# Expert outputs added to X's rows in DRAM by an indirect DMA, instead of stored, gathered and added by VectorE

## The chip, the cores and the metric

The kernel runs on one core of one Trainium2 chip. The metric is device microseconds of one execution, the median of three runs.

## The reference

A two-layer trunk over x (1024 tokens by 1024 features, float32). Each layer has a mixer and then a mixture of experts:

```python
x = x + g1[:, None, :] * y                        # y: the mixer's output
h = modulate(rms_norm(x, norm_ffn_g[l]), sh2, sc2)
x = x + g2[:, None, :] * grouped_moe(h, ...)
# grouped_moe: 16 experts, each token goes to 2 of them with gates summing to 1
a = silu(t @ w_gate[e]) * (t @ w_up[e])           # 1024 -> 256
y = sum over the token's 2 experts of gate * (a @ w_down[e])
```

Behind layer 0's experts stands layer 1's mixer: RMS norm of x, modulation, and a 1024 to 2048 projection `w1` with a gated activation, a width-31 convolution, and so on. Behind layer 1's experts stands the final RMS norm and the output.

## The kernel before

X stays in on-chip memory, 128 partitions by 8 blocks of 1024 features; block b holds tokens 128b to 128b+127. Engines are programmed one by one and wait on semaphores; there is no planner, so each engine's own order is the order of its work.

**The expert stage.** The router gives each token two slots. Slots are grouped by expert and padded to tiles of 128, so `nt` tiles are run a layer. `TOKI` holds for each tile and partition the token of that slot. Per tile:

- POOL gathers the tile's 128 normalised rows from `xn_scratch` in DRAM into `XG` with an indirect DMA (L581), for tile t+1 as soon as TensorE has transposed tile t (semaphore `xtr`); `XG` is a single buffer.
- TensorE's loop body for tile t is, in this order: gate and up of tile t (L1005, 16 records), transposes of tile t+1 (L996, waits for the gather), down of tile t-1 (L1020), transposes of tile t's hidden rows (L1012).
- ScalarE and VectorE evict the transposes, VectorE multiplies (L1161), and `tile_out` (L1419, L1421) scales the down result by the slot's gate and by g2 into the single buffer `YS`. It waits until the previous content of `YS` has left (`y_out`).
- ScalarE's queue stores `YS` to `y_scratch` at the tile's place (L691).
- SP's queue loads the weights of the expert three ahead, 3 MB, when the buffer's last `down` is done (L439 to L441).

**The combine.** When all tiles are stored, POOL issues 16 indirect gathers (L607), two for each block, and VectorE adds each to X (`combine`). ScalarE takes sums of squares block by block (`rms_sums`, L651), and after four blocks a root; VectorE normalises (`rms_apply`, L1227, L1231); TensorE transposes a half of 512 tokens (L869), ScalarE and VectorE evict (`evict_ht`). Only when both halves are there does TensorE start `w1`'s 16 groups (L886; group n takes `w1_group(n)`, whose first two need the first half only). In layer 1 two roots of four blocks each stand before the output.

SP loads the first two `w1` weight pieces when the last `down` of layer 0 is done, and two more when the last gather has landed.

Of the kernel before, what the change touches and what calls it, by code (L numbers as in the profile page):

```python
# [15 lines left out]
P = 128  # L16
# [108 lines left out]
def emptied(g):  # L125

    return CONSUMER[:g + 1].count(CONSUMER[g])


def trunk(nc, i, out):  # L130
    with ExitStack() as ctx:
# [35 lines left out]
        TCUR = sb("TCUR", [P, 1], U32)  # L167
        RT = sb("RT", [1, 5 * MAXT], I32)
# [73 lines left out]
        def hv(n):  # L242
            return HTR[:, n, :]

        Y1, Y2 = ([HTR[:, 3 * n + b, :] for b in range(3)] + [R[:, 3 - n, b * D:(b + 1) * D] for b in range(4)]
                  for n in range(2))
        NY0, NY = 3, 7

        def y_of(b):

            return b if b < NY else NY0
# [11 lines left out]
        xn_dram = nc.dram_tensor("xn_scratch", (T, D), F32, kind="Internal").ap()  # L263
        y_dram = nc.dram_tensor("y_scratch", (MOST * P, D), F32, kind="Internal").ap()
# [38 lines left out]
        xup = sem("x_updated")  # L303
# [40 lines left out]
        c_in = [[[sem(f"combine_in{l}_{b}_{s}") for s in range(2)] for b in range(NB)] for l in range(NL)]  # L344
# [66 lines left out]
        def _(sp):  # L411
# [54 lines left out]
            sp.wait_ge(zeroed, 16 * (NH + 1))  # L466
            nt = experts(0)
            sp.wait_ge(dn[0], nt)
# [23 lines left out]
            for n in range(2):  # L492
                weights1(n)
# [6 lines left out]
            sp.wait_ge(c_in[0][NB - 1][1], 16)  # L500
# [10 lines left out]
            experts(1)  # L511
# [7 lines left out]
        def _(pool):  # L519
# [35 lines left out]
            rest = y_dram[LEAST * P:MOST * P, :].rearrange("(t p) d -> p t d", p=P)  # L555
            zeros = ZERO.unsqueeze(1).broadcast_to([P, MOST - LEAST, HT])

            for q in range(16):
                if q == 4:
                    for h in range(NH):  # L560
                        pool.dma_start(rest[:, :, HT * h:HT * h + HT], zeros).then_inc(zeroed, 16)
                    pool.dma_start(glu_dram.rearrange("(c p) t -> p c t", p=P)[:, :, 0:PADC],
                                   ZERO[:, 0:KC * PADC].rearrange("p (c t) -> p c t", c=KC)).then_inc(zeroed, 16)
                l, s = q // 8, (2, 5)[q // 4 % 2]
                n = 24 * l + 4 * s + q % 4
                pool.wait_ge(ada_fin, n + 1)
                pool.dma_start(g_dram[q // 4:q // 4 + 1, q % 4 * QW:(q % 4 + 1) * QW], BROW[q % NBROW]
                               ).then_inc(brow_out[q % NBROW], 16)

            for l in range(NL):  # L570
# [13 lines left out]
                pool.tensor_tensor(PSCR[:, l:l + 1], PSCR[:, 2:3], PSCR[:, 2:3], ALU.add).then_inc(held[l], 1)  # L584
                pool.tensor_copy(TCUR[:], TOKI[:, 0:1]).then_inc(cur_ok[l], 1)
                pool.wait_ge(cur_ok[l], 1)
                gather()
                with pool.Fori(0, nt) as t:
# [4 lines left out]
                    pool.wait_ge(held[l], t + 1)  # L593

                    pool.tensor_tensor(PSCR[:, l:l + 1], PSCR[:, 2:3], PSCR[:, 2:3], ALU.add).then_inc(held[l], 1)
                    gather()

                pool.wait_ge(zeroed, 16 * (NH + 1))
                pool.wait_ge(y_out[l], nt * 16 + 16)
                pool.wait_ge(xg_in[l], nt * 16 + 16)  # L600
                pool.wait_ge(held[l], nt + 1)
                pool.tensor_tensor(PSCR[:, l:l + 1], PSCR[:, 2:3], PSCR[:, 2:3], ALU.add).then_inc(held[l], 1)
# [22 lines left out]
        def _(act):  # L625
# [18 lines left out]
            def rms_sums(r, h):  # L644

                if r == 0:
                    act.wait_ge(xl[h], 16)
                for b in range(4 * h, 4 * h + 4):
                    if r:
                        act.wait_ge(xup, 8 * (r // 2 - 1) + b + 1)  # L650
# [17 lines left out]
            def experts(l):  # L668
# [13 lines left out]
                act.sem_inc(y_out[l], 16)  # L682
# [6 lines left out]
                def store(t):  # L689
                    act.wait_ge(ys_d[l], t + 2)  # L690
                    act.dma_start(y_dram[bass.ds(t * P, P), :], YS).then_inc(y_out[l], 16)  # L691
                hidden(0)
                with act.Fori(1, nt) as t:
                    hidden(t)
                    store(t - 1)
                store(nt - 1)
# [59 lines left out]
            for h in range(NH):  # L756
                rms_sums(2, h)
            for h in range(NH):
                evict_ht(2, 1, 0, h)
            for n in range(16):  # L760
# [4 lines left out]
                act.activation(SIG[n % 2], take(g)[:], ACT.Sigmoid,  # L765
                               bias=PT[:, COL_B1 + KC + ct:COL_B1 + KC + ct + 1]).then_inc(free["A"], 1)
            act.wait_ge(conv_ok, KC)
# [24 lines left out]
            rms_sums(4, 0)  # L792
            rms_sums(4, 1)
# [3 lines left out]
        def _(pe):  # L797
# [294 lines left out]
            transposes(2, 1)  # L1092
# [31 lines left out]
            for n in range(16):  # L1124
                c, h = w1_group(n)
                ht_ready(2, h)
# [24 lines left out]
        def _(dve):  # L1151
# [68 lines left out]
            def rms_apply(r, h):  # L1220
# [4 lines left out]
                for b in range(4 * h, 4 * h + 4):  # L1225
                    if r < 4:
                        dve.tensor_scalar(XN[h][:, b % 4, :], X[:, b, :], RSTD[:, b:b + 1], None,  # L1227
                                          ALU.mult).then_inc(xn_ok, 1)
                        continue
                    dve.wait_ge(small_in, 48)  # L1230
                    dve.scalar_tensor_tensor(out=OUTS[b], in0=X[:, b, :], scalar=RSTD[:, b:b + 1],  # L1231
                                             in1=FGB, op0=ALU.mult, op1=ALU.mult).then_inc(out_ok, 1)
# [22 lines left out]
            def route(l):  # L1255
# [74 lines left out]
                for s, oh in ((0, OH1), (1, OH2)):  # L1330
# [12 lines left out]
                                              op0=ALU.mult, op1=ALU.add))  # L1343
                q3 = [P, 16, MAXT]
# [3 lines left out]
                for s in range(TOPK):  # L1348
# [4 lines left out]
                    tt(q4[:, s], q4[:, s], TOKF[:].unsqueeze(2).broadcast_to([P, NB, MAXT]), ALU.mult)  # L1353
# [33 lines left out]
                dve.tensor_copy(TOKI[:], X0[:, 0:MAXT]).then_inc(tab_ok, 1)  # L1387
# [192 lines left out]
            for b in range(NB):  # L1580
                if b == 5:
                    rms_apply(2, 0)
                combine(0, b)
            evict_ht(2, 1, 0, 0)
            rms_apply(2, 1)
            evict_ht(2, 1, 0, 1)
            for n in range(16):
                c, h = w1_group(n)
                g = GROUPS["w1"] + 2 * n + 1
                dve.wait_ge(free["A"], emptied(g - 1))  # L1590
# [38 lines left out]
            experts(1)  # L1629
            for b in range(NB):  # L1630
                if b == 5:
                    rms_apply(4, 0)
                combine(1, b)
            rms_apply(4, 1)
# [23 lines left out]
```

## Time and profile before

| | |
|---|---|
| median of 3 runs | 1817.98 us |
| lowest, highest | 1814.69, 1820.83 us |
| span of the profiled execution | 1812.5 us |
| TensorE busy | 1533.8 us, 85% |
| VectorE busy | 856.0 us, 47% |
| POOL busy | 150.2 us, 8% |

No time apart from the span is given for the profiled execution; the median of the runs is 5.5 us above that span. Times in the trace count from the span's start. PE is TensorE, DVE is VectorE, ACT is ScalarE, POOL is GpSimd; a q behind the name is that engine's queue of DMA issues. PEclk is the share of full clock granted to TensorE.

### The profile page before, as it was taken

Reading aid. Unit: us, or ns where it says so; the run is one execution under the profiler, and the core shown is the slowest. Engines: PE = TensorE matmul, PEld = TensorE weight load, DVE = VectorE, ACT = ScalarE, POOL = GpSimd, SP = SyncE. Lnnn points to the kernel's source line nnn. Section 1 sums busy time; section 2 is a strip of 40 time slices with the busy share of each in tenths; the row PEclk is TensorE's granted clock in tenths of the full one; section 3 lists DMA queues with packets and bytes.
Section 4 is the critical chain, followed back from the end, with each engine's and each line's share of the span. In section 5 each row is a group of like instructions: output and inputs, shape, how many; then the busy total and the mean of one; then the engine's idle time right before and its main releaser. Section 6 shows DMA issues by size and latency. Waiting matters only on the chain.

```text
span 1812.5 us, 17004 instructions
## 1 busy us (share of the span) xinstructions
PE 1533.8 (85%) x5355; PEld 850.0 (47%) x5356; DVE 856.0 (47%) x1548; ACT 258.0 (14%) x507; POOL 150.2 (8%) x267
## 2 busy tenths in 40 slices
PE   3799999989955999999359989987997489999980
PEld 2684544458843444444134334432886344444430
DVE  3554686644243332232353999966224422223326
ACT  2210000001121111111130000005112011111112
POOL 2000000000000111011310000000001011011104
PEclk9999999999986999999769989998999599999995
DMA  9574066560143666794532335442004567556727
GB/s 334 160 279 154 25 217 210 169 202 1 47 181 121 231 221 219 268 327 155 189 128 65 99 91 131 105 107 81 1 1 163 186 221 281 200 189 238 281 80 280
DMA packets 196430, 300.79 MB, mean 166 GB/s; under 512 B 12021, under 2 KB 153425, under 8 KB 196384
## 3 DMA queue, kind: packets, MB, share of 16 engines
q1 hardware_dynamic: 169952, 205.94, 36.1%
q0 software_dynamic: 17696, 62.24, 9.5%
q10 hardware_dynamic: 8736, 31.99, 4.5%
q8 instruction: 30, 0.49, 0.1%
q14 instruction: 16, 0.13, 0.0%
HBM read 248.51 MB, written 51.53 MB: 166 GB/s over the span
## 4 chain that ended last, share of the span: by engine, by line
PE 63%; DMA 16%; DVE 13%; issue 2%; ACT 2%; SPq 1%; POOL 1%; DVEq 0%; POOLq 0%; ACTq 0%
PE bank L886 19%; PE bank L964 15%; PE bank L1005 13%; DMA W<-in_moe_w_down 12%; PE bank L1020 6%; DVE W L1183 3%; DVE R L1604 3%; PE bank L996 2%; DVE R L1161 2%; PE bank L1109 1%; DMA W<-in_ada_w 1%; PE bank L869 1%; DVE X L1161 1%; PE bank L1142 1%; PE bank L903 1%
## 5 line engine op out<-in xcount | busy, mean ns | idle before, releaser
L886 PE MATMUL bank<-HTR,W 128*128 128x512 f32 x1024 | 451.4, 599 | 7.2 <-DVE R L1591 7.2
L1005 PE MATMUL bank<-W,R 128*128 (+1 forms) x816 | 369.5, 606 | 31.0 <-DMA W<-in_moe_w_down 14.2
L886 PEld LDWEIGHTS bank<-HTR,W 128*128 128x128 f32 x1024 | 193.9, 192 | 244.6 <-issue 244.0
L1161 DVE TENSOR_TENSOR R<-bank,R 128x256 f32<-128x256 f32 (+1 forms) x91 | 49.3, 542 | 540.6 <-ACT R L686 339.0
L1005 PEld LDWEIGHTS bank<-W,R 128*128 128x128 f32 x816 | 153.0, 192 | 217.8 <-issue 213.8
L964 PE MATMUL bank<-W,R 128*128 128x256 f32 x1024 | 231.1, 385 | 9.0 <-ACT R L786 7.8
L964 PEld LDWEIGHTS bank<-W,R 128*128 128x128 f32 x1024 | 194.6, 193 | 38.6 <-ACT R L786 8.7
L1604 DVE SCALAR_TENSOR_TENSOR R<-R,PT 128x998 f32<-128x998 f32 (+21 forms) x152 | 195.1, 1284 | 5.4
L1020 PE MATMUL bank<-W,R 128*128 x408 | 187.1, 602 | 3.8 <-DVE R L1412 3.8
L1183 DVE SCALAR_TENSOR_TENSOR W<-W,CAB 128x256 f32<-128x256 f32 x308 | 149.3, 485 | 11.0
L1020 PEld LDWEIGHTS bank<-W,R 128*128 128x128 f32 x408 | 74.7, 193 | 79.7 <-issue 79.7
L1419 DVE SCALAR_TENSOR_TENSOR R<-bank,GSLOT,HTR 128x512 f32<-128x512 f32 x51 | 38.3, 750 | 123.4 <-PE bank L1020 123.4
L678 ACT ACTIVATE R<-bank,MC 128x128 f32<-128x128 f32 x212 | 79.9, 457 | 95.4 <-PE bank L996 95.4
L686 ACT ACTIVATE R<-bank 128x256 f32<-128x256 f32 x51 | 19.6, 385 | 494.0 <-PE bank L1005 494.0
L869 PE MATMUL bank<-IDENT,R 128*128 128x128 f32 x128 | 27.4, 378 | 63.6 <-DVE R L1227 45.7
L1395 DVE TENSOR_SCALAR R<-bank,MC 128x128 f32<-128x128 f32 x212 | 72.4, 403 | 18.2 <-PE bank L996 18.2
L1161 DVE TENSOR_TENSOR R<-R 128x512 f32<-128x512 f32 (+8 forms) x146 | 64.5, 462 | 24.6 <-ACT R L751 21.3
L996 PEld LDWEIGHTS bank<-IDENT,R 128*128 128x128 f32 x424 | 50.9, 144 | 42.5 <-issue 26.9
L996 PE MATMUL bank<-IDENT,R 128*128 128x128 f32 x424 | 56.8, 278 | 15.2 <-DMA R<-xn_scratch,TCUR 15.2
L964 PE MATMUL bank<-W,HTR 128*128 128x256 f32 x256 | 58.7, 388 | 2.4 <-ACT HTR L660 1.4
L869 PEld LDWEIGHTS bank<-IDENT,R 128*128 128x128 f32 x128 | 20.6, 193 | 72.4 <-issue 35.0
L581 POOL DMA_INDIRECT R<-xn_scratch,TCUR x53 | 52.1, 983 | 25.1 <-issue 24.2
(191 smaller groups left out, 945.6 us busy)
## 6 DMA issues: line engine op xcount, KB each, us to landing
W<-in_ada_w SPq DMA_DIRECT2D x48, 1024.0 KB, 11.6
W<-in_moe_w_gate SPq DMA_DIRECT2D x32, 1024.0 KB, 7.4
W<-in_moe_w_up SPq DMA_DIRECT2D x32, 1024.0 KB, 11.0
W<-in_moe_w_down SPq DMA_DIRECT2D x32, 1024.0 KB, 12.9
y_scratch<-R ACTq DMA_DIRECT2D x51, 512.0 KB, 7.5
W<-glu_scratch SPq DMA_DIRECT2D x48, 258.0 KB, 4.6
W<-in_conf_w SPq DMA_DIRECT2D x12, 1024.0 KB, 8.8
W<-in_hyb_w_in SPq DMA_DIRECT2D x10, 1024.0 KB, 12.9
```

What stands on the lines that cost most here:

```text
L581: return pool.indirect_dma_start(out=XG, out_offset=None, in_=xn_dram, in_offset=bass.IndirectOffsetOnAxis(ap=TCUR[:, 0:1], axis=0)).then_ ...
L678: ins = act.activation(XT[:, k, :], TB_[0][:, k * P:(k + 1) * P], ACT.Identity, bias=MC[:, l, 3, k:k + 1], scale=MC[:, l, 2, k:k + 1])
L869: ins = pe.transpose(TB_[q % 2][:, P * b:P * b + P], XN[h][:, b, P * k:P * k + P], IDENT[:])
L886: ins = pe.matmul(dst[:], lhs(k), rhs(k), start=(k == 0), stop=(k == kc - 1))
L964: ins = pe.matmul(dst[:, QW * b:QW * b + QW], src[:, k, t0:t0 + P], w[:, k, :], start=(k == 0), stop=(k == KC - 1))
L996: ins = pe.transpose(TB_[k // 4][:, P * (k % 4):P * (k % 4) + P], XG[:, P * k:P * k + P], IDENT[:])
L1005: ins = pe.matmul(M[0][:], XT[:, k, :], W[:, bass.ds(at + k * 2 * FE, 2 * FE)], start=(k == 0), stop=(k == KC - 1))
L1020: ins = pe.matmul(M[1 + h][:], AT[:, k, :], W[:, bass.ds(at + 2 * KC * FE + k * D + h * HT, HT)], start=(k == 0), stop=(k == 1))
L1161: return dve.tensor_tensor(o, a, b, op)
L1183: ins = dve.scalar_tensor_tensor(out=acc, in0=w[:, k, :], scalar=CAB[:, k, 0:1], in1=acc, op0=ALU.mult, op1=ALU.add)
L1395: ins = dve.tensor_scalar(XT[:, k, :], TB_[1][:, (k - 4) * P:(k - 3) * P], MC[:, l, 2, k:k + 1], MC[:, l, 3, k:k + 1], ALU.mult, ALU.add)
L1604: link(dve.scalar_tensor_tensor(out=o[:, d:T], in0=p[:, 0:T - d], scalar=tap(CTAPS - 1 - d), in1=o[:, d:T], op0=ALU.mult, op1=ALU.add))
```

## The change

`y_scratch` and its zero fill go. In their place `xsum_scratch` (`xs_dram`) holds a copy of X's rows: ScalarE stores four pieces of 1 MB while the mixer's output projection finishes. For each tile POOL issues an indirect DMA that adds `YS` onto the 128 rows of `xs_dram` that the tile's tokens name. This `add_rows(t - 1)` stands in POOL's loop behind `next_tile(t)`, which issues the gather of tile t+1. It waits for the previous add to have landed and for `tile_out`. Padding slots name a spare block of rows.

When the last add has landed, SP reloads X in eight blocks of 512 KB. The combine, its gathers and the `xup` semaphore are gone. Behind layer 0, SP loads the first two `w1` pieces after four of the eight reloads, and the transposes and evictions of the second half stand behind `w1`'s first two groups. Behind layer 1, root, scaling and output go block by block.

```diff
 # POOL, setup: the zero fill of y_scratch goes, a spare block of rows stays
-            rest = y_dram[LEAST * P:MOST * P, :].rearrange("(t p) d -> p t d", p=P)
-            zeros = ZERO.unsqueeze(1).broadcast_to([P, MOST - LEAST, HT])
...
+                        pool.dma_start(xn_dram[T:T + P, s], ZERO).then_inc(zeroed, 16)
+                        pool.dma_start(xs_dram[T:T + P, s], ZERO).then_inc(y_out[h], 16)
 # POOL, the expert stage
+                def next_tile(t):
                     pool.wait_ge(xg_in[l], t * 16 + 16)
                     pool.tensor_copy(TCUR[:], TOKI[:, bass.ds(t + 1, 1)]).then_inc(cur_ok[l], 1)
                     pool.wait_ge(cur_ok[l], t + 2)
                     pool.wait_ge(xtr[l], t + 1)
+                    met()
                     gather()
+                def add_rows(t):
+                    pool.wait_ge(y_out[l], t * 16 + 16)
+                    pool.tensor_copy(TSUM[:], TOKI[:, bass.ds(t, 1)]).then_inc(sum_cur[l], 1)
+                    pool.wait_ge(sum_cur[l], t + 1)
+                    pool.wait_ge(ys_d[l], t + 2)
+                    met()
+                    pool.indirect_dma_start(
+                        out=xs_dram, out_offset=bass.IndirectOffsetOnAxis(ap=TSUM[:, 0:1], axis=0),
+                        in_=YS, in_offset=None, compute_op=ALU.add).then_inc(y_out[l], 16)
...
+                next_tile(0)
+                pool.wait_ge(x_out[l], 16 * 4)
+                with pool.Fori(1, nt) as t:
+                    next_tile(t)
+                    add_rows(t - 1)
+                add_rows(nt - 1)
-                for b in range(NB):
-                    if b == NY:
-                        pool.wait_ge(xup, 8 * l + NY0 + 1)
-                    for s, dst in ((0, Y1), (1, Y2)):
-                        pool.indirect_dma_start(
-                            out=dst[y_of(b)], out_offset=None, in_=y_dram,
-                            in_offset=bass.IndirectOffsetOnAxis(ap=SLOTU[:, s, b:b + 1], axis=0)
-                        ).then_inc(c_in[l][b][s], 16)
 # ACT
-                def store(t):
-                    act.wait_ge(ys_d[l], t + 2)
-                    act.dma_start(y_dram[bass.ds(t * P, P), :], YS).then_inc(y_out[l], 16)
 # ACT, x_pieces: four stores a layer of X's rows, 1 MB each
+                    act.dma_start(xs_dram[2 * P * p:2 * P * (p + 1), :].rearrange("(b q) d -> q b d", q=P),
+                                  X[:, 2 * p:2 * p + 2, :]).then_inc(x_out[l], 16)
 # SP
+            def reload(l, nt, b):
+                if b == 0:
+                    sp.wait_ge(y_out[l], nt * 16 + 16)
+                sp.dma_start(X[:, b, :], xs_dram[P * b:P * b + P, :]).then_inc(x_back[b], 16)
-            sp.wait_ge(dn[0], nt)
...
-            for n in range(2):
-                weights1(n)
+            for b in range(NB):
+                reload(0, nt, b)
+                if b == 3:
+                    for n in range(2):
+                        weights1(n)
...
-            sp.wait_ge(c_in[0][NB - 1][1], 16)
...
-            experts(1)
+            nt = experts(1)
+            for b in range(NB):
+                reload(1, nt, b)
 # PE, ACT and DVE: the second half's transposes move behind the first two groups of w1
             transposes(2, 0)
-            transposes(2, 1)
             for n in range(16):
                 c, h = w1_group(n)
+                if n == 2:
+                    transposes(2, 1)
 # DVE, route: padding slots name rows T + p of the spare block, each its own
+                tokr = SM[:, 0:16].rearrange("p (s b) -> p s b", s=TOPK)
+                link(dve.tensor_scalar(SPARE[:], TOKF[:, 0:1], float(T), None, ALU.add))
+                for s in range(TOPK):
+                    dve.scalar_tensor_tensor(out=tokr[:, s, :], in0=TOKF[:], scalar=-float(T),
+                                             in1=rf.rearrange("p (s b) -> p s b", s=TOPK)[:, s, :],
+                                             op0=ALU.add, op1=ALU.subtract).then_inc(dch, 1)
...
-                dve.tensor_copy(TOKI[:], X0[:, 0:MAXT]).then_inc(tab_ok, 1)
+                dve.tensor_scalar(TOKI[:], X0[:, 0:MAXT], SPARE[:], None, ALU.add).then_inc(tab_ok, 1)
 # DVE, behind the experts
-            def combine(l, b):
-                for s, y in ((0, Y1), (1, Y2)):
-                    dve.wait_ge(c_in[l][b][s], 16)
-                    ins = tt(X[:, b, :], X[:, b, :], y[y_of(b)], ALU.add)
-                    if s == 0:
-                        link(ins)
-                ins.then_inc(xup, 1)
+            def last_norm(b):
+                dve.wait_ge(fin_sd, b + 1)
+                link(dve.reciprocal(RSTD[:, b:b + 1], SD[:, b:b + 1]))
+                dve.scalar_tensor_tensor(out=OUTS[b], in0=X[:, b, :], scalar=RSTD[:, b:b + 1],
+                                         in1=FGB, op0=ALU.mult, op1=ALU.mult).then_inc(out_ok, 1)
```

## Rows read from the trace of the kernel before

**Rows 1.** The page: the span, and TensorE's line of busy times.

```profile
span 1812.5 us, 17004 instructions
PE 1533.8 (85%) x5355; PEld 850.0 (47%) x5356; DVE 856.0 (47%) x1548; ACT 258.0 (14%) x507; POOL 150.2 (8%) x267
```

**Rows 2.** Busy time by stretch: 12 us of layer 0's expert stage.

```profile
core 0: us, PE busy (x) PEld busy (x) DVE busy (x) ACT busy (x) POOL busy (x), PEclk, DMA share, GB/s
648.00:660.00 12.00, 11.69 (x36) 5.62 (x35) 3.49 (x8) 1.89 (x5) 1.35 (x3) 1.00 1.00 349
```

**Rows 3.** Timeline, one tile: start us, us, engine, line, operation, count, [idle before].

```profile
649.64 1.04 PE L996 MATMUL bank<-IDENT,R 128*128 128x128 f32 x8
...
650.51 3.60 PE L1020 MATMUL bank<-W,R 128*128 x8
...
650.81 0.18 POOL L595 TENSOR_TENSOR PSCR<-PSCR 1x1 f32<-1x1 f32 x1 [6.72 <-PE bank L996]
651.46 0.98 POOL L581 DMA_INDIRECT R<-xn_scratch,TCUR  x1 [0.46 <-issue]
...
654.36 0.75 DVE L1419 SCALAR_TENSOR_TENSOR R<-bank,GSLOT,HTR 128x512 f32<-128x512 f32 x1 [2.28 <-PE bank L1020]
...
655.03 0.74 DVE L1421 SCALAR_TENSOR_TENSOR R<-bank,GSLOT,HTR 128x512 f32<-128x512 f32 x1
...
655.95 0.34 ACTq L691 DMA_DIRECT2D y_scratch<-R  x1
656.91 0.18 POOL L590 COPY TCUR<-TOKI 128x1 uint32 x1 [4.47 <-DMA R<-xn_scratch,TCUR]
661.61 0.60 PE L996 MATMUL bank<-IDENT,R 128*128 128x128 f32 x4
```

**Rows 4.** DMA issues: count, KB, median us to landing; then the landings of L581.

```profile
y_scratch<-R ACTq DMA_DIRECT2D x51, 512.0 KB, 7.5
...
R<-xn_scratch,TCUR POOLq DMA_INDIRECT x53, 4.5
...
DMA to landing us min/median/max: 4.0/4.5/7.6
```

**Rows 5.** The chain: gate-and-up of tile 1 and of the last tile, each layer.

```profile
582.81 7.13 PE bank L1005 x16
...
860.66 7.13 PE bank L1005 x16
...
1453.13 7.13 PE bank L1005 x16
...
1744.61 7.13 PE bank L1005 x16
```

**Rows 6.** Behind layer 0's experts: timeline, and last the chain.

```profile
880.54 0.74 DVE L1421 SCALAR_TENSOR_TENSOR R<-bank,GSLOT,HTR 128x512 f32<-128x512 f32 x1
...
907.50 1.06 ACT L651 ACTIVATE R<-X 128x1024 bf16<-128x1024 f32 x1 [2.64 <-DVE X L1161]
...
913.64 1.94 PE L869 MATMUL bank<-IDENT,R 128*128 128x128 f32 x8 [34.02 <-DVE R L1227]
...
933.55 6.62 PE L869 MATMUL bank<-IDENT,R 128*128 128x128 f32 x28 [3.77 <-DVE R L1227]
...
941.06 41.22 PE bank L886 x96
```

**Rows 7.** Behind layer 1's experts: timeline and chain.

```profile
1764.49 0.74 DVE L1421 SCALAR_TENSOR_TENSOR R<-bank,GSLOT,HTR 128x512 f32<-128x512 f32 x1
...
1765.41 2.67 DMA y_scratch<-R
```

**Rows 8.** Busy time by stretch, columns as in rows 2: two gaps of TensorE.

```profile
578.00:583.00 5.00, 1.57 (x12) 1.10 (x11) 2.05 (x6) 1.89 (x5) 1.16 (x2) 1.00 0.29 93
872.40:874.20 1.80, 0.00 (x0) 0.00 (x0) 1.69 (x3) 0.00 (x0) 0.00 (x0) 1.00 0.00 0
874.20:879.70 5.50, 5.39 (x8) 2.03 (x8) 0.00 (x0) 0.00 (x0) 0.00 (x0) 0.69 0.23 95
```

More of the change, by code:

```diff
@@ L167, in trunk @@
         TCUR = sb("TCUR", [P, 1], U32)
+        TSUM = sb("TSUM", [P, 1], U32)
+        SPARE = sb("SPARE", [P, 1])
         RT = sb("RT", [1, 5 * MAXT], I32)
@@ L243, in hv @@
             return HTR[:, n, :]
[L245 to L251, printed above, removed]
         GBF = hv(6)
@@ L260, in trunk @@
         X0, X1 = bank[6], bank[7]
-        xn_dram = nc.dram_tensor("xn_scratch", (T, D), F32, kind="Internal").ap()
-        y_dram = nc.dram_tensor("y_scratch", (MOST * P, D), F32, kind="Internal").ap()
+        xn_dram = nc.dram_tensor("xn_scratch", (T + P, D), F32, kind="Internal").ap()
+        xs_dram = nc.dram_tensor("xsum_scratch", (T + P, D), F32, kind="Internal").ap()
         g_dram = nc.dram_tensor("gate_scratch", (4, D), F32, kind="Internal").ap()
@@ L302, in trunk @@
         gb_in = [sem(f"gate_rows_in{n}") for n in range(4)]
-        xup = sem("x_updated")
         dch = sem("dve_step")
@@ L343, in trunk @@
         y_out = [sem(f"tile_stored{l}") for l in range(NL)]
-        c_in = [[[sem(f"combine_in{l}_{b}_{s}") for s in range(2)] for b in range(NB)] for l in range(NL)]
+        x_out = [sem(f"x_rows_stored{l}") for l in range(NL)]
+        x_back = [sem(f"x_block_reloaded{b}") for b in range(NB)]
+        sum_cur = [sem(f"sum_tokens_copied{l}") for l in range(NL)]
+        fin_sd = sem("final_root_ready")
         out_ok = sem("output_block_ready")
@@ L466, in _ @@
             sp.wait_ge(zeroed, 16 * (NH + 1))
+            for l in range(NL):
+                sp.wait_ge(y_out[l], 16)
+            def reload(l, nt, b):
+                if b == 0:
+                    sp.wait_ge(y_out[l], nt * 16 + 16)
+                sp.dma_start(X[:, b, :], xs_dram[P * b:P * b + P, :]).then_inc(x_back[b], 16)
             nt = experts(0)
-            sp.wait_ge(dn[0], nt)
             def weights1(n):
@@ L560, in _ @@
                     for h in range(NH):
-                        pool.dma_start(rest[:, :, HT * h:HT * h + HT], zeros).then_inc(zeroed, 16)
+                        s = slice(HT * h, HT * h + HT)
+                        pool.dma_start(xn_dram[T:T + P, s], ZERO).then_inc(zeroed, 16)
+                        pool.dma_start(xs_dram[T:T + P, s], ZERO).then_inc(y_out[h], 16)
                     pool.dma_start(glu_dram.rearrange("(c p) t -> p c t", p=P)[:, :, 0:PADC],
@@ L583, in gather, with met @@
                         in_offset=bass.IndirectOffsetOnAxis(ap=TCUR[:, 0:1], axis=0)).then_inc(xg_in[l], 16)
[L584 to L588, printed above, removed]
+                def met():
+                    pool.tensor_tensor(PSCR[:, l:l + 1], PSCR[:, 2:3], PSCR[:, 2:3], ALU.add).then_inc(held[l], 1)
+                def next_tile(t):
                     pool.wait_ge(xg_in[l], t * 16 + 16)
@@ L592, in _ @@
                     pool.wait_ge(xtr[l], t + 1)
-                    pool.wait_ge(held[l], t + 1)
-                    pool.tensor_tensor(PSCR[:, l:l + 1], PSCR[:, 2:3], PSCR[:, 2:3], ALU.add).then_inc(held[l], 1)
+                    met()
                     gather()
-                pool.wait_ge(zeroed, 16 * (NH + 1))
-                pool.wait_ge(y_out[l], nt * 16 + 16)
-                pool.wait_ge(xg_in[l], nt * 16 + 16)
-                pool.wait_ge(held[l], nt + 1)
-                pool.tensor_tensor(PSCR[:, l:l + 1], PSCR[:, 2:3], PSCR[:, 2:3], ALU.add).then_inc(held[l], 1)
-                for b in range(NB):
-                    if b == NY:
-                        pool.wait_ge(xup, 8 * l + NY0 + 1)
-                    for s, dst in ((0, Y1), (1, Y2)):
-                        pool.indirect_dma_start(
-                            out=dst[y_of(b)], out_offset=None, in_=y_dram,
-                            in_offset=bass.IndirectOffsetOnAxis(ap=SLOTU[:, s, b:b + 1], axis=0)
-                        ).then_inc(c_in[l][b][s], 16)
+                def add_rows(t):
[7 more added lines that the diff above has]
+                        in_=YS, in_offset=None, compute_op=ALU.add).then_inc(y_out[l], 16)
+                met()
+                pool.tensor_copy(TCUR[:], TOKI[:, 0:1]).then_inc(cur_ok[l], 1)
+                pool.wait_ge(cur_ok[l], 1)
+                gather()
+                next_tile(0)
[4 more added lines that the diff above has]
+                add_rows(nt - 1)
+                pool.wait_ge(xg_in[l], nt * 16 + 16)
                 if l == 0:
@@ L649, in rms_sums @@
                     if r:
-                        act.wait_ge(xup, 8 * (r // 2 - 1) + b + 1)
+                        act.wait_ge(x_back[b], 16 * (r // 2))
                     link(act.activation(JUNK, X[:, b, :], ACT.Square, accum_out=SS[:, b:b + 1]))
@@ L681, in experts @@
                 evict_tile(1)
-                act.sem_inc(y_out[l], 16)
                 def hidden(t):
@@ L694, in experts @@
                     hidden(t)
-                    store(t - 1)
-                store(nt - 1)
             def x_pieces(l, g0):
@@ L754, in _, with gate1 @@
             experts(0)
[L756 to L760, printed above, removed]
+            def gate1(n):
                 g = GROUPS["w1"] + 2 * n
@@ L766, in _ @@
                                bias=PT[:, COL_B1 + KC + ct:COL_B1 + KC + ct + 1]).then_inc(free["A"], 1)
+            rms_sums(2, 0)
+            evict_ht(2, 1, 0, 0)
+            rms_sums(2, 1)
+            for n in range(16):
+                if n == 2:
+                    evict_ht(2, 1, 0, 1)
+                gate1(n)
             act.wait_ge(conv_ok, KC)
@@ L791, in _ @@
             experts(1)
-            rms_sums(4, 0)
-            rms_sums(4, 1)
+            for b in range(NB):
+                act.wait_ge(x_back[b], 32)
+                link(act.activation(JUNK, X[:, b, :], ACT.Square, accum_out=SS[:, b:b + 1]))
+                act.activation(SD[:, b:b + 1], SS[:, b:b + 1], ACT.Sqrt, bias=EPSC[:],
+                               scale=1.0 / D).then_inc(fin_sd, 1)
         @block.tensor
@@ L1125, in _ @@
                 c, h = w1_group(n)
+                if n == 2:
+                    transposes(2, 1)
                 ht_ready(2, h)
@@ L1225, in rms_apply @@
                 for b in range(4 * h, 4 * h + 4):
[L1226 to L1232, printed above, removed]
+                    dve.tensor_scalar(XN[h][:, b % 4, :], X[:, b, :], RSTD[:, b:b + 1], None,
+                                      ALU.mult).then_inc(xn_ok, 1)
             def evict_ht(r, l, ffn, h, ks=range(1, KC, 2)):
@@ L1343, in route @@
                                               op0=ALU.mult, op1=ALU.add))
+                tokr = SM[:, 0:16].rearrange("p (s b) -> p s b", s=TOPK)
[4 more added lines that the diff above has]
+                                             op0=ALU.add, op1=ALU.subtract).then_inc(dch, 1)
+                    steps[0] += 1
                 q3 = [P, 16, MAXT]
@@ L1352, in route @@
                     dve.wait_ge(dch, steps[0])
-                    tt(q4[:, s], q4[:, s], TOKF[:].unsqueeze(2).broadcast_to([P, NB, MAXT]), ALU.mult)
+                    tt(q4[:, s], q4[:, s], tokr[:, s, :].unsqueeze(2).broadcast_to([P, NB, MAXT]), ALU.mult)
                 tt(RO, IOTA[:].unsqueeze(1).broadcast_to([P, 16, P]),
@@ L1578, in _ @@
             experts(0)
[L1580 to L1583, printed above, removed]
+            rms_apply(2, 0)
             evict_ht(2, 1, 0, 0)
             rms_apply(2, 1)
-            evict_ht(2, 1, 0, 1)
             for n in range(16):
@@ L1589, in _ @@
                 g = GROUPS["w1"] + 2 * n + 1
+                if n == 2:
+                    evict_ht(2, 1, 0, 1)
                 dve.wait_ge(free["A"], emptied(g - 1))
@@ L1629, in _ @@
             experts(1)
+            dve.wait_ge(small_in, 48)
             for b in range(NB):
[L1631 to L1634, printed above, removed]
+                last_norm(b)
 INPUTS = ["x", "c", "ada_w", "ada_b", "norm_mix_g", "norm_ffn_g", "hyb_w_in", "sgu_ln_g", "sgu_ln_b",
```

## The prediction

> **What bounds the kernel now.** I read the page first: TensorE is busy for 1533.8 of 1812.5 us [rows 1]. Then I took busy time by stretch. In the expert stage TensorE is all but full: 11.69 us of 12 at full clock, while POOL has 1.35 us of work [rows 2]. So the stage is bound by TensorE's own order of work, and anything that makes it wait once a tile costs once a tile.
>
> The timeline of one tile shows the slack that the change spends. TensorE transposes a tile at 649.64. POOL sees it at 650.81 and issues the next gather at 651.46, before the down of the tile is done. It has landed when POOL goes on at 656.91, and TensorE comes back for it at 661.61 [rows 3]: 4.7 us of slack. The store of `YS` is issued at 655.95 and lands in 7.5 us [rows 4], 663.4. VectorE wants the buffer again one period after 654.36, at about 666.3, which leaves 2.9 us.
>
> The period comes from the chain: 582.81 to 860.66 in 23 steps, and 1453.13 to 1744.61 in 24 [rows 5], together 569.3 us in 47 steps, 12.1 us each. The store's count is 51 [rows 4], so the layers have 25 and 26 tiles.
>
> Behind each expert stage the kernel is bound by a string of dependent work: 881.3 (end of the last `tile_out`) to 941.06 (first `w1` matmul) is 59.8 us in layer 0 [rows 6], and 1765.2 to the span's end at 1812.5 is 47.3 us in layer 1 [rows 1, 7]. This is what the change shortens.
>
> **What the change saves, layer 0.** The last `tile_out` still ends at 881.3. POOL then needs a wake-up, `met` and a pause: 0.13 + 0.18 + 0.47 = 0.78 us, as between the end of the transposes and the gather [rows 3]. The add is issued at 882.1. No accumulating DMA is in the trace. Below, the nearest row is the plain store of the same bytes with the queues empty, 2.67 us [rows 7]; above, the gather's longest landing, 7.6 [rows 4]. I take 5.0, near an indirect transfer's usual 4.5: landed at 887.1. The reloads follow. I take 2.7 us to the first landing (the same store) and then 1.5 us a block, since 0.524 MB at the 349 GB/s that the queues reach [rows 2] is 1.5. Block 3 is in at 887.1 + 2.7 + 4.5 = 894.3. From the start of that block's sum of squares to the first transpose takes 913.64 - 907.50 = 6.1 us [rows 6]: 900.4. A half of transposes with its evictions takes 941.06 - 933.55 = 7.5: 907.9. By then two pieces of `w1` (2 MB more, 6 us) are in as well, at about 900.3. Two groups of `w1` are two thirds of 41.22 us, 27.5 [rows 6]: 935.4. Now the second half's transposes, 7.5, and the third group, 13.7: 956.6. Before, the third group ended at 941.06 + 41.22 = 982.3. VectorE's convolution work starts there, and that work sets the pace next, so this is the point to compare. Saved: 25.7 us; from 20 (add 7.6, reload paced at two thirds of the rate) to 28 (add 2.7).
>
> **Layer 1.** The add is issued at 1765.2 + 0.8 = 1766.0 and lands at 1771.0. Eight loads and eight output stores of 0.524 MB are 8.4 MB, 24 us at 349 GB/s. The last store's landing adds some 2: the end is at 1797, 15.5 us earlier, from 11 to 19. Sum of the savings: 41 us.
>
> **Small items.** The four 1 MB stores of X fall under the projection, where TensorE has work and the queues little; I price them at nothing, and 3 us a layer (1 MB at 349 GB/s) if the last one delayed the rows that the first gather reads. The three more VectorE steps in the router are on the path, small ones, for which POOL's smallest of 0.18 us [rows 3] is the nearest row: under 1 us a layer. The removed zero fill ran beside TensorE's first projections and frees nothing that anyone waits for. Together +1 us.
>
> **What it costs in the loop.** POOL's order is now gather(t+1), add(t-1), gather(t+2). Add(t-1) must wait for `tile_out(t-1)`, that is for down(t-1), which TensorE does *after* transposing t+1. So gather(t+2), so far issued right behind the transposes, is now held behind down, `tile_out` and the issue of the add. The loop that closes, counted from the start of the transposes:
> - to the start of `tile_out`: 654.36 - 649.64 = 4.72
> - `tile_out`: 655.03 + 0.74 - 654.36 = 1.41
> - POOL wake-up, `met`, pause: 0.78
> - issue of the add, as the gather's: 0.98 (bounds half and twice that; no row shows this form)
> - end of the loop, copy to `TCUR`, `met`, pause: estimated at 1.25, from two small operations of 0.18, 0.47 of pause, and some 0.4 between them and for the branch
> - sum to the gather's issue: 9.1 us [rows 3]
> - gather to landing: L
> - and TensorE starts the next transposes.
>
> The period is 9.1 + L, where it used to be 12.1. L was 4.0 to 7.6, median 4.5 [rows 4], when the gather started ahead of the weights. Now it starts in their midst and right behind the add of the same size on its own queue. The store that started at that moment took 7.5. I take 7.5 for the 26 tiles beside a weight load (16 experts a layer, three of them loaded ahead of the loop) and 5.1 for the other 21: mean 6.4. Bounds 4.0 and 12 (below, the slow add).
>
> TensorE then idles some 4 us a tile. After 1.8 us without work the clock was granted at 0.69 over the next 5.5 us, and the eight `down` records in it took 5.39 us [rows 8] in place of 3.60 [rows 3]. But in 578 to 583, with 1.57 of 5 us busy, it stayed at 1.00 [rows 8]. The transposes and `down` behind the gap are on the closed loop. I take half of 5.39 - 3.60 = 1.8: 0.9; bounds 0 and the rival below. The Trainium skill has a rule for this (*TensorE: Matmul & The Clock Gate*, section "HAM oscillation — how this bites in real kernels"): idle gaps once an iteration make the array start each one at the low clock. By it every tile would pay; the two gaps here agree once and once not.
>
> Period: 9.1 + 6.4 + 0.9 = 16.4, that is 4.3 more. Adds stand ahead of the gathers of tiles 3 to nt, nt - 2 periods a layer: 23 + 24 = 47. 47 x 4.3 = 202 us. The wait of `tile_out` for the previous add stays hidden: it has 16.4 - 2.2 = 14.2 us. The weights have more room than before.
>
> **Sum.** +202 - 41 + 1 = +162 us. From the profiled span, 1812.5 + 162 = 1974.5; with the 5.5 us by which the median lies above it, **1980 us**. The savings are worth 41 / 47 = 0.87 us a tile: the loop decides.
>
> **The rivals.**
> 1. *Only the order costs.* The add and the weights don't slow the gather, L = 4.5, and the clock holds. For it: landings keep near 4.5 beside weights in most tiles. Against: the store's 7.5 at just this moment. Period 13.6, +71 - 40 = +31: 1849 us.
> 2. *The clock falls every tile.* At the low level eight transposes take 1.94 us [rows 6] against 1.04 [rows 3], 0.9 more, and down 1.8 more: 2.7 in place of 0.9. Period 18.2, +287 - 40: 2065 us. This is the page's rule in the rows' numbers.
> 3. *The adding DMA itself is slow.* If it needs 12 us, 1.6 times the busy store's 7.5 [rows 4], and the gather lands 1.3 us behind it, the period is 6.9 + 12 + 1.3 + 0.9 = 21.1, +423, and each layer's savings shrink by 7: +397, 2215 us. For it: it must read its target and write it. The Trainium skill (*Collectives: The Full Stack*, "The bandwidth ceiling: the fold count and why AG ≠ RS ≠ AR") says that a reducing transfer runs at about half rate, since it reads two sources; by that alone the add's 1.5 us of transfer would be 3, an estimate, and no run here shows it.
> 4. *The other side: the gather stays hidden.* It needs 9.1 + L at 12.1 or less. If POOL came to the gather 1.1 us sooner than I counted and L were its shortest 4.0, nothing would stall, and the savings stand: 1818 - 41 = 1777 us. It decides for faster when the period stays below 12.1 + 0.87 = 13.0. Against: 9.1 is nearly all measured rows, and 4.0 is the minimum of 53 gathers that had nothing ahead of them.
>
> **How the numbers follow.** Forecast 0.44 (own range 1910 to 2045, L from 5 to 7.5 with its clock share); rival 1 0.16; rival 2 0.19; rival 3 0.16; rival 4 0.05. A change within 0.3%, some 5 us, is what a measurement of this kernel can't tell from none: it needs a period of 12.9 to 13.1, 0.02 of rival 4. Slower 0.95, same 0.02, faster 0.03. Range: from rival 1 with a little less L, 1845, to short of the slow add, 2165; outside lie rival 4 and most of rival 3.
>
> **What would show it.** Right: TensorE's idle time ahead of L996, released by the gather, 3 to 6 us a tile where it is now none; gates-and-ups some 16.4 us apart; the gather issued at about 9.1 us behind the transposes, right behind the add; PEclk below 1.00 in parts of the stage; 51 adds. Also the first `w1` matmul 26 us after the last `tile_out` and not 60, and some 32 us from the last `tile_out` to the end. Wrong: gates-and-ups still 12 us apart; or the wait found at `tile_out` for the add, not at the transposes; or an add whose issue takes many us on POOL.

## The result, and the profile after

The changed kernel takes 2107.18 us (median of 4 runs, 2104.51 to 2110.3) against 1819.4 for the kernel before (median of 4 here); the ratio is 1.159, interval 1.1568 to 1.1611. It is 288 us slower. I had said 162 us slower, 1980 us, range 1845 to 2165.

The page of the changed kernel, span and TensorE:

```profile
span 2108.5 us, 17096 instructions
PE 1611.2 (76%) x5355; PEld 890.8 (42%) x5356; DVE 819.4 (39%) x1528; ACT 259.0 (12%) x513; POOL 215.6 (10%) x388
```

TensorE runs the same 5355 instructions as in [rows 1], takes 77 us more for them, and is idle the rest of the added 296 us of span. The list of waits says for what, with total us, times, and the longest (PEld is TensorE's loading of weights, which waits for the same rows just ahead of it):

```profile
POOL PSCR L593 <- DVE R L1443: 497.0, 51, 16.8
...
PEld bank L1014 <- DMA R<-xn_scratch,TCUR: 327.4, 49, 9.1
...
PE bank L1014 <- DMA R<-xn_scratch,TCUR: 288.2, 49, 8.3
```

The first line is POOL standing in `add_rows` until `tile_out` is done; the other two are TensorE at the transposes, where it waits for the gather. Before the change that wait was there twice, for each layer's first tile.

The timeline of two tiles, the answer to [rows 3]:

```profile
665.41 1.73 PE L1014 MATMUL bank<-IDENT,R 128*128 128x128 f32 x8 [3.35 <-DMA R<-xn_scratch,TCUR]
666.93 4.69 PE L1038 MATMUL bank<-W,R 128*128 x8
...
672.54 0.74 DVE L1443 SCALAR_TENSOR_TENSOR R<-bank,GSLOT,HTR 128x512 f32<-128x512 f32 x1
672.91 1.96 SPq L438 DMA_DIRECT2D W<-in_moe_w_down  x1
...
674.11 1.61 POOL L611 DMA_INDIRECT xsum_scratch<-R,TSUM  x1 [0.50 <-issue]
...
676.35 1.02 POOL L588 DMA_INDIRECT R<-xn_scratch,TCUR  x1 [0.16 <-issue]
...
684.34 0.18 POOL L607 COPY TSUM<-TOKI 128x1 uint32 x1 [6.97 <-DMA xsum_scratch<-R,TSUM]
686.67 1.97 PE L1014 MATMUL bank<-IDENT,R 128*128 128x128 f32 x8 [7.96 <-DMA R<-xn_scratch,TCUR]
```

Read it as one closed loop: transposes at 665.41, down, `tile_out` done at 673.28, add issued at 674.11, gather at 676.35, and TensorE goes on when it has landed, at 686.67, after 7.96 us idle. In [rows 3] the gather left 1.8 us behind the start of the transposes; here it leaves 10.9 us behind.

Landings of the gather, then of the add (min, median, max), against 4.0/4.5/7.6 in [rows 4]:

```profile
DMA to landing us min/median/max: 4.1/6.2/10.6
...
DMA to landing us min/median/max: 6.1/9.8/10.5
```

From one gate-and-up to the next, tile 1 to the last of each layer, the timeline gives 582.38 to 1022.83 and 1596.45 to 2053.56: 897.6 us in the 47 steps that took 569.3 in [rows 5], 19.1 us each, +328 us. The steps have two sizes: 26 of 21.4 us on average, where a weight load is in flight, and 21 of 16.2. TensorE stands idle ahead of the transposes for 7.9 us on average in the long ones and 3.0 in the short ones.

Busy time by stretch over one step of each size, then over 400 us of each layer's expert stage, the answer to [rows 2] (columns as there):

```profile
655.03:671.68 16.65, 13.30 (x37) 6.51 (x35) 3.53 (x8) 1.89 (x5) 3.38 (x6) 0.90 0.30 63
671.68:692.67 20.99, 13.03 (x37) 6.60 (x35) 3.52 (x8) 1.89 (x5) 3.38 (x6) 0.84 0.64 200
...
600.00:1000.00 400.00, 272.66 (x688) 132.44 (x686) 70.99 (x161) 38.18 (x101) 68.85 (x122) 0.85 0.52 154
1600.00:2000.00 400.00, 278.27 (x712) 137.02 (x711) 72.94 (x166) 39.70 (x105) 67.60 (x120) 0.85 0.50 147
```

The granted clock is below 1.00 in all of them, and TensorE's work, 11.69 us a tile before, takes 13.

What the change was to save is there too. Behind layer 0's experts, timeline, and in the last two lines the chain:

```profile
1048.70 0.74 DVE L1443 SCALAR_TENSOR_TENSOR R<-bank,GSLOT,HTR 128x512 f32<-128x512 f32 x1
...
1049.88 1.59 POOL L611 DMA_INDIRECT xsum_scratch<-R,TSUM  x1 [0.16 <-issue]
1056.11 1.77 SPq L470 DMA_DIRECT2D X<-xsum_scratch  x4
...
1059.75 1.06 ACT L666 ACTIVATE R<-X 128x1024 bf16<-128x1024 f32 x1 [24.21 <-DMA X<-xsum_scratch]
...
1078.12 27.71 PE bank L904 x64
...
1112.40 13.99 PE bank L904 x32
```

From the end of the last `tile_out` (1049.44) to the end of `w1`'s third group (1126.39) it is 76.9 us, where [rows 6] give 982.28 - 881.28 = 101.0: 24.1 us saved. In layer 1 the last `tile_out` ends at 2078.4 and the span at 2108.5, 30.1 us against the 47.3 of [rows 1, 7]: 17.2 saved. The last `tile_out` itself comes later: from the last gate-and-up to its end it is 26.6 and 24.8 us, before 20.6 in both layers, 10 us given back. Sum: +328 - 41 + 10 = +297, and the spans differ by 296. (The medians differ by 288: the profiled execution was the shortest of the four before, and the longest of the four after.)

### The profile page after: what moved, and what is told of

Same layout as the page of the kernel before. It is cut to its first block and busy times, and to the rows that moved or that the text cites. A ratio compares the mean times of both kernels' runs of the same rounds, so it can differ in the third digit from the quotient of the medians.

```text
span 2108.5 us, 17096 instructions
## 1 busy us (share of the span) xinstructions
PE 1611.2 (76%) x5355; PEld 890.8 (42%) x5356; DVE 819.4 (39%) x1528; ACT 259.0 (12%) x513; POOL 215.6 (10%) x388
## 5 line engine op out<-in xcount | busy, mean ns | idle before, releaser
L1014 PE MATMUL bank<-IDENT,R 128*128 128x128 f32 x424 | 89.2, 379 | 288.2 <-DMA R<-xn_scratch,TCUR 288.2
L1038 PE MATMUL bank<-W,R 128*128 x408 | 236.3, 733 | 3.8 <-DVE R L1434 3.8
L1023 PEld LDWEIGHTS bank<-W,R 128*128 128x128 f32 x816 | 154.2, 194 | 189.4 <-issue 185.4
L982 PEld LDWEIGHTS bank<-W,R 128*128 128x128 f32 x1024 | 194.3, 192 | 38.5 <-ACT R L801 8.7
L1038 PEld LDWEIGHTS bank<-W,R 128*128 128x128 f32 x408 | 97.5, 253 | 110.2 <-issue 108.9
L611 POOL DMA_INDIRECT xsum_scratch<-R,TSUM x51 | 82.3, 1613 | 26.2 <-issue 26.2
L593 POOL TENSOR_TENSOR PSCR<-PSCR 1x1 f32<-1x1 f32 x104 | 19.0, 183 | 571.8 <-DVE R L1443 497.0
L887 PE MATMUL bank<-IDENT,R 128*128 128x128 f32 x128 | 24.6, 346 | 42.8 <-DVE R L1246 32.5
```

The lines of the kernel that those rows point to most:

```text
L611: pool.indirect_dma_start(out=xs_dram, out_offset=bass.IndirectOffsetOnAxis(ap=TSUM[:, 0:1], axis=0), in_=YS, in_offset=None, compute_op=A ...
L982: ins = pe.matmul(dst[:, QW * b:QW * b + QW], src[:, k, t0:t0 + P], w[:, k, :], start=(k == 0), stop=(k == KC - 1))
L1014: ins = pe.transpose(TB_[k // 4][:, P * (k % 4):P * (k % 4) + P], XG[:, P * k:P * k + P], IDENT[:])
L1023: ins = pe.matmul(M[0][:], XT[:, k, :], W[:, bass.ds(at + k * 2 * FE, 2 * FE)], start=(k == 0), stop=(k == KC - 1))
L1038: ins = pe.matmul(M[1 + h][:], AT[:, k, :], W[:, bass.ds(at + 2 * KC * FE + k * D + h * HT, HT)], start=(k == 0), stop=(k == 1))
```

## The experiments

My theory: TensorE waits for a gather that POOL's order makes late (order), and that lands late (it queues behind the add and beside the weights); the clock adds to it. The rivals: the adding DMA as such is the load; the weights; the clock. For each run I read the mean step from the timeline like above, since it isn't touched by what a run leaves out elsewhere. "Landing" is the time from a transfer's issue to its arrival.

**The order turned (e1).** POOL issues the gather of tile t+2 ahead of the add of tile t-1:

```diff
+                next_tile(1)
                 with pool.Fori(1, nt) as t:
-                    next_tile(t)
+                    next_tile(t + 1)
                     add_rows(t - 1)
+                pool.wait_ge(xg_in[l], nt * 16 + 32)
                 add_rows(nt - 1)
-                pool.wait_ge(xg_in[l], nt * 16 + 16)
```

> The changed kernel, with POOL's loop turned: the gather of tile t+2 is issued before the add of tile t-1, so it is no longer held behind down, tile_out and the add's issue. My theory (TensorE waits each tile for a gather that the order makes late): no idle time ahead of the transposes is left, the gather lands some 5 us after its issue, and the period falls from 19.1 us back to between 12.1 (as before the change) and 12.6 (tile_out 1.4 + wake-up 0.8 + the add's longest landing 10.5), so 47 x 6.5 to 7.0 us go: 1775 to 1805 us. Rival (the adding DMA itself is the load, whatever the order): the wait moves to tile_out, the period stays at 14 us or more, 1870 us or more.

Measured: 1790.45 us, ratio to the kernel before 0.9854 (0.9816 to 0.9892). Its timeline:

```profile
649.85 1.04 PE L1015 MATMUL bank<-IDENT,R 128*128 128x128 f32 x8
...
651.69 1.02 POOL L588 DMA_INDIRECT R<-xn_scratch,TCUR  x1 [0.47 <-issue]
...
655.18 0.75 DVE L1442 SCALAR_TENSOR_TENSOR R<-bank,GSLOT,HTR 128x512 f32<-128x512 f32 x1 [2.89 <-DMA xsum_scratch<-R,TSUM]
...
657.42 1.61 POOL L611 DMA_INDIRECT xsum_scratch<-R,TSUM  x1 [0.50 <-issue]
...
661.84 1.04 PE L1015 MATMUL bank<-IDENT,R 128*128 128x128 f32 x8
```

The gather leaves 1.8 us behind the transposes again and TensorE has no idle time ahead of them. `tile_out` now does wait for the previous add in about half of the tiles, as the rival had it: it starts 0.1 to 2.0 us later behind the start of down than in the kernel before (3.85 us), and TensorE doesn't feel it. The step is 12.45 us (585.3 in 47). So 312 of the 328 us hang on that order, with the adding DMA left as it is. The other 16 come from 8 steps of 13.6 to 16.3 us, where weights come late; the remaining 39 take 11.97 us on average:

```profile
766.50 8.83 PE L1024 MATMUL bank<-W,R 128*128 x16 [4.20 <-DMA W<-in_moe_w_down]
```

The last piece of an expert's weights lands in a median of 14.2 us in this run, against 12.9 in the kernel before. Not all of the 16 us can be put down to the adds, though: e9 below has no adds and an expert stage like that of the kernel before, and its profiled run has 8 such steps too, of 13.4 to 14.9 us, and 577.8 us in 47 steps, where the kernel before has 4 and 569.3. There the last piece lands in 13.1. That the adds' traffic delays the weights further fits these numbers; no run shows it by itself.

The same kernel again (e8), next to the two that follow:

> The same kernel as e1_gather_first, on the same chip as e5 and e9, for a narrower interval: 1785 to 1795 us, ratio to the kernel before 0.982 to 0.989.

Measured: 1790.64 us, ratio 0.9862 (0.9838 to 0.9886), step 12.43 us.

**No add (e2).** The gather's late place alone:

```diff
-                    pool.indirect_dma_start(
-                        out=xs_dram, out_offset=..., in_=YS, in_offset=None, compute_op=ALU.add)
+                    pool.dma_start(xs_dram[T:T + 16, 0:16], YS[0:16, 0:16]).then_inc(y_out[l], 16)
```

> The changed kernel with a plain 1 KB store in the place of each tile's add, so that the expert outputs are left out of X; POOL's order and all waits stay. It prices the order alone. My theory (order, and the queueing behind the add on top): the gather is issued some 8.5 us behind the transposes, lands in 4.5 to 6.5, TensorE still waits, the period is 13.5 to 15.5 us, 1850 to 1945 us. Rival (the weights, not the add, make the gather slow): landing stays at 10 us beside a weight load, period about 18, 2050 us.

Measured: 1929.56 us (one run), step 15.73, just above the band of my theory: 17.9 beside weights and 13.0 elsewhere.

```profile
677.59 0.56 POOL L611 DMA_DIRECT2D xsum_scratch<-R  x1 [0.25 <-issue]
...
678.85 1.02 POOL L588 DMA_INDIRECT R<-xn_scratch,TCUR  x1 [0.23 <-issue]
...
686.90 1.77 PE L1012 MATMUL bank<-IDENT,R 128*128 128x128 f32 x8 [4.47 <-DMA R<-xn_scratch,TCUR]
```

With nothing of size ahead of it on its queue the gather still needs 8.0 us in the midst of a weight load (the same in the median of those steps), and 4.3 elsewhere. The rival was right about this half: weights alone take it from 4.3 to 8, though not to 10. It was wrong in the sum, since the order with the weights accounts for 3.6 of the 7.0 us a step.

**A plain scatter (e3).** `compute_op=ALU.add` is dropped, so rows are overwritten. This also changes layer 1's routing to 24 tiles, so steps are to be compared, not the time.

> The changed kernel with the indirect DMA writing its rows instead of adding them (X's old rows are overwritten, the sum is left out). It prices the read of the target alone. Theory A (the read makes the add slow and the gather queues behind it): the add's landing falls from 9.8 to about 7.5 us, the gather's beside weights from 10 to about 8, period 17, about 2010 us. Theory B (bytes written and order decide, the read is free): landings and time stay within 1%, 2090 to 2125 us.

Measured: 1986.94 us (one run), step 17.43 (784.5 us in 45): 20.3 beside weights and 13.5 elsewhere. Theory A holds in direction: the landing falls from 9.8 to 7.5 us in the median of all, that of the gather beside weights from 10.2 to 9.4 only. So adding instead of writing costs 2.7 us in the steps without weights and 1.1 in those with. Of the 2.7, 0.6 is the longer issue and 1.2 the gather's landing behind it (5.6 against 4.4); the rest goes with the clock, since here TensorE's idle time ahead of the transposes is only 1.2 us in these steps, and they take 1.09 us there, next to the 1.04 of full clock. That it is the read of the target which costs is argued: the run only takes the adding away. POOL's side of it:

```profile
653.31 1.00 POOL L611 DMA_INDIRECT xsum_scratch<-R,TSUM  x1 [0.49 <-issue]
...
654.93 1.00 POOL L588 DMA_INDIRECT R<-xn_scratch,TCUR  x1 [0.15 <-issue]
...
656.82 0.18 POOL L607 COPY TSUM<-TOKI 128x1 uint32 x1 [0.90 <-DMA xsum_scratch<-R,TSUM]
```

The scatter lands in 3.5 us without weights, the add in 6.2 (1049.88 to 1056.11 above); beside weights the medians are 8.5 and 10.0. Issuing takes 1.00 us against 1.61.

**Light weights (e6).** From the fourth expert on, an eighth or less of each weight load, so those experts compute mostly with the weights that lay in the buffer before.

```diff
-                sp.dma_start(wgu[:, :, 0:FE], pick(g)).then_inc(s, 16)
+                sp.dma_start(wgu[:, 0:1, 0:FE], pick(g)[:, 0:1, :]).then_inc(s, 16)
```

and so for the other two of each expert; for the first three experts the full loads stay.

> The changed kernel (POOL's order as there) with an eighth or less of each weight load from the fourth expert on, so the outputs of those experts are wrong. It takes the weights out of the queues. Theory (the gather's landing is 10 us beside a weight load and 6 us without one): all steps are 15.4 to 16.9 us, the two-valued pattern goes, 2107 - 47 x 2.7 = 1980 us, plus or minus 20. Rival (the add alone makes some gathers slow): 21 us steps remain, 2060 us or more.

Measured: 1974.96 us (one run). All of layer 0's steps from the third tile on are 15.2 to 17.2 us, mean over both layers 16.14. The long steps are the weights' doing. Landings of the gather:

```profile
DMA to landing us min/median/max: 4.1/5.5/6.1
```

**The gap filled (e4, e7).** Extra matmuls into an unused bank ahead of the transposes keep TensorE busy where it would wait:

```diff
                     gate_up(t, expert_at(t), thr)
+                    for k in range(FILL):              # 4 in e4, 8 in e7
+                        pe.matmul(M[3][:], XT[:, k, :], X[:, 0, 0:HT],
+                                  start=(k == 0), stop=(k == FILL - 1))
                     transpose_tile(t * 16 + 32)
```

> The changed kernel with 4 extra matmuls of 512 columns (8 records, 3.4 us) into an unused bank between gate-and-up and the transposes, where TensorE waits for the gather. Theory (the gap costs the clock, and transposes and down behind it run partly at the low level): PEclk in the stage rises to about 1.00, transposes take 1.04 us and not 1.97, down 3.6 and not 4.2 to 5.7, the period falls by 1.5 to 2.5 us, 1990 to 2040 us. Rival (the clock costs nothing on this path): time stays at 2107, or rises where the gap is shorter than 3.4 us, by up to 10 us.

Measured: 2093.41 us (one run), a gain of 14 us where I had expected at least 67. The steps without weights fell from 16.2 to 15.5, and have no idle time left ahead of the transposes, so that here the filler itself is in the way; those with weights stayed at 21.4, as 3.6 to 4.8 us of idle time were left in them:

```profile
686.11 1.97 PE L1015 MATMUL bank<-IDENT,R 128*128 128x128 f32 x8 [3.89 <-DMA R<-xn_scratch,TCUR]
687.87 5.70 PE L1039 MATMUL bank<-W,R 128*128 x8
```

> The changed kernel with 8 extra matmuls of 512 columns (16 records, 6.9 us) in the place where e4_fill had 4. Theory (in the 8 us gaps beside a weight load four were too few to hold the clock): PEclk near 1.00, steps beside a weight load fall from 21.2 to about 19.3, and the others rise from 16.6 to some 18.7, as TensorE is then full: 2085 to 2110 us in all. Rival (the clock is not what lengthens these steps): the former stay at 21, in all 2140 us or more.

Measured: 2127.36 us (one run), between the two bands that I had set. The clock is at 1.00, and even the long steps now have transposes and down at full speed:

```profile
600.00:1000.00 400.00, 386.18 (x1032) 177.34 (x1031) 74.07 (x168) 39.59 (x105) 71.06 (x126) 1.00 0.53 157
...
656.62 1.09 PE L1015 MATMUL bank<-IDENT,R 128*128 128x128 f32 x8 [0.87 <-DMA R<-xn_scratch,TCUR]
657.63 3.70 PE L1039 MATMUL bank<-W,R 128*128 x8
```

The long steps are 19.9 us, 1.5 less than 21.4; the others are bound by the filler at 18.3. So the clock costs 1.5 us in long steps. In short ones it costs at least the 0.8 of e4, which the filler cuts short; from the start of the transposes to the next gather's issue it is 10.7 us on average in the changed kernel and 9.3 in e4's short steps, so 1.3 is nearer. That is some 1.4 on average: part of the loss, and not its cause.

**The deferral (e5, e9).** Two runs ask how much of the saving behind layer 0 is the moved transposes. In e5 they are put back into e1; in e9 they alone are put into the kernel before. The edit of e9, here for TensorE, with the evictions likewise (e5 undoes it in e1):

```diff
             transposes(2, 0)
-            transposes(2, 1)
             for n in range(16):
+                if n == 2:
+                    transposes(2, 1)
```

> The kernel that gathers first (e1), with the second half's transposes and evictions put back ahead of w1's first group. It prices the deferral alone. Theory: in e1 the second half's normalised rows are ready at 927.7 us and TensorE started w1 at 920.6; undone, w1's third group starts at about 927.8 + 7.3 + 27.5 = 962.6 in place of 954.9, 7.7 us later, so 1794 to 1801 us against e1's 1790. Rival (the deferral only moves the wait, since the convolution behind is bound elsewhere): within 2 us of e1.

> The kernel before, with only the deferral of the second half's transposes (stores, gathers and VectorE's adds stay). It tells how much of the saving behind layer 0 needs the change at all. Theory: w1 starts at about 930.7 in place of 941.1, the transposes then cost 6.7 us in the middle, so the third group starts at 964.9 in place of 968.5: 3 to 4 us saved, ratio 0.998, inside or at the edge of what can be told. Rival (the deferral is the source of the 24 us saved there): 1795 us or less.

Measured: e5 1802.75 us, ratio 0.9916 (0.9893 to 0.9939), 12 us above e8 of the same session. The expectation had 7.7; the mean step of the profiled run is also 0.1 longer, 5 us in 47 steps, in a stage that the edit doesn't touch, so 7 are the deferral's. The traces agree: from the end of the last `tile_out` to the end of `w1`'s third group it is 84.0 us in e5 and 76.9 in e8. e9 1811.83 us, ratio 0.998 (0.9961 to 0.9998), as expected: 4 us by the medians, and 5.3 by that stretch in its trace (95.7 against 101.0). So of the 24 us behind layer 0 about 7 are the deferral, and the kernel before could have had some 4 or 5 of them without the change. No run takes the savings of layer 1 apart into the reload and the output block by block.

## Why the prediction was right, and where its size was off

The direction, the place and the mechanism were as forecast: TensorE waits at the transposes, once a tile, for a gather that stands behind `tile_out` and the add. Turning POOL's order takes the wait away (e1). The number is another matter: 2107 us lies inside the wide range but outside the forecast's own 1910 to 2045, and the loss in the loop came out 1.6 times what I had added up. By the forecast's own terms:

- *To the gather's issue, 9.1 us.* At full clock it was 9.4: in the step whose transposes begin at 1001.68 the gather is issued at 1011.10. (With the clock as it was granted the median is 10.9.) The issue of the add and the way to the gather were together 2.23 us, as priced, though otherwise divided: the issue takes 1.6, and the way behind it only 0.6.

```profile
1001.68 1.09 PE L1014 MATMUL bank<-IDENT,R 128*128 128x128 f32 x8 [3.18 <-DMA R<-xn_scratch,TCUR]
...
1008.87 1.61 POOL L611 DMA_INDIRECT xsum_scratch<-R,TSUM  x1 [0.50 <-issue]
1009.91 0.77 POOL L598 COPY TCUR<-TOKI 128x1 uint32 x1
...
1011.10 1.02 POOL L588 DMA_INDIRECT R<-xn_scratch,TCUR  x1 [0.15 <-issue]
```

- *L, 6.4 us. This is the term that was mis-sized.* I took 7.5 beside weights and 5.1 elsewhere. The two tiles above show 10.3 (676.35 to 686.67) and 5.7 (659.69 to 665.41), the medians are 10.2 and 5.6, the mean over 47 is 8.2: 1.8 of the 2.7 us by which the step of 19.1 exceeds my 16.4. I read the store's 7.5 as the price of a transfer in the midst of the weights, which e2 bears out (8.0), but did not put the add on top of it. The medians of the gather's landing beside weights take it apart: 8.0 with a 1 KB store ahead of it (e2), 9.4 with the plain scatter ahead (e3), 10.2 with the add.
- *The clock, 0.9 us.* Some 1.4 by e4 and e7, at least 1.2; the full rival (2.7) did not come about. With 9.4 and 8.2 that makes 19.0 of the 19.1 measured.
- *47 steps.* As counted; 26 with weights, as counted.
- *Loss in the loop, 202 us.* 328: 7.0 a step and not 4.3.
- *Small items, 1 us.* Nothing to be seen: the first gate-and-up of layer 0 starts at 567.6 us, before at 567.9.
- *Savings, 41 us.* 41.3, 24.1 and 17.2 against 25.7 and 15.5. The add landed in 6.2 and not 5.0, and the first reload in 3.6 and not 2.7, which the rest made good.
- *Not in the sum:* the last tiles. The last `tile_out` has no long step ahead of it to hide the previous add, and waits for it 2.7 us (it starts 6.6 us behind the start of down, where at full clock it is 3.95); with the wait of 3 us for one more gather before the last two downs, and what follows it, this is 10 us in both layers together.

Of the rivals, "the clock falls every tile" was closest in time (2065 us), by luck: its own term is 1.4 us and not 2.7, and what made up the difference is the gather's landing. "The adding DMA itself is slow" (2215) is half of the truth: it lands in 9.8 us in the median and not 12. "Only the order costs" (1849) holds in the steps without weights of e2 (13.0 us, forecast 13.6), and fails beside weights, which slow the gather to 8.0 us with next to no add; e2 takes 1930 us. "The gather stays hidden" is refuted in this order, and is what e1 gives: I had put its time at 1777 us, and it comes to 1790, because some weights come later.

The Trainium skill's rule on a reducing transfer (*Collectives: The Full Stack*, "The bandwidth ceiling: the fold count and why AG ≠ RS ≠ AR"), half rate for reading two sources, is stated for ReduceScatter in a ring of cores, another transfer than this one. It speaks in the right direction: 6.2 us to landing against the scatter's 3.5. By the Trainium skill's rule on idle gaps (*TensorE: Matmul & The Clock Gate*, "HAM oscillation — how this bites in real kernels") each iteration behind such a gap starts at the low clock. The trace agrees for the 26 long steps, where the transposes take 1.97 us each time, and only in part for the 21 short ones, where they take from 1.04 to 1.97. Over the stage the granted clock is 0.85, and 1.00 when the gap is filled (e7).

## What to carry to other kernels

A queue that issues for two stages of a pipeline must issue in the order in which their inputs become ready; one that waits for the later stage ahead of the earlier closes a loop through TensorE, VectorE, itself and the DMA, and the loop's length is the sum of every latency in it. Before putting a DMA behind another wait, write down what its engine issues next and who waits for that. And price a landing by the traffic it will meet at its new time, what is just ahead of it on its own queue included: here the same gather took 4.5, 5.7, 8.0 and 10.3 us.

Of the versions here e1 is the fastest, 1790 us, 1.4% below the kernel before. A second `YS` buffer, so that `tile_out` need not wait for the add, was not tried.

## What the runs showed of the hardware

- An indirect DMA that adds 128 rows of 4 KB in DRAM took POOL 1.61 us to issue, where the same without the add took 1.00, and landed 6.2 us after its issue with the weights out of the way, against 3.5.
- Behind the add's issue (1.61 us from 1008.87) the record of the small copy to `TCUR` starts early, at 1009.91, but takes 0.77 us and ends 0.20 us behind the end of the issue. Behind the scatter's issue in e3 the same copy starts at its end (654.32), takes 0.19 and also ends 0.20 behind it. So the early start gains nothing.
- Beside a weight load the add landed in 10.0 us in the median and the scatter in 8.5 (8.6 in the one from 666.49 to 675.13 in e3): adding instead of writing cost 1.5 us of landing there, and 2.9 where no weights were in flight (medians 6.2 and 3.4).
- With the weights in flight an indirect gather of 128 rows of 4 KB landed in 8.0 us (e2, nothing of size ahead of it), and in 4.3 without them.
